# The last expert job of a hybrid decoder step on its own, and the work behind it

## What is computed

```python
def moe_swiglu(x, w_r, wg, wu, wd):
    logits = (x @ w_r).astype(jnp.float32)
    top_v, top_i = lax.top_k(logits, TOP_K)
    gates = jax.nn.softmax(top_v, axis=-1)
    dense_gate = jnp.sum(jax.nn.one_hot(top_i, N_EXPERTS, dtype=jnp.float32) * gates[..., None], axis=-2)
    out = jnp.zeros_like(x)
    for e in range(N_EXPERTS):
        out = out + dense_gate[..., e:e + 1].astype(x.dtype) * swiglu(x, wg[e], wu[e], wd[e])
    return out
    ...
    y = rmsnorm(x, P['ln_final'])
```

## Time and profile before

| | us |
|---|---|
| median of three runs | 1769.19 (1766.17 to 1771.72) |
| profiled execution | 1768.95 |
| its span | 1767.2 |
| TensorE busy | 1711.3 (97%) |
| VectorE busy | 1360.0 (77%) |
| ScalarE busy | 1054.7 (60%) |
| GpSimd busy | 111.5 (6%) |

### The profile page before, as it was taken

One profiled execution on the slowest core, in us unless ns is written; L12 is line 12 of the kernel. 1 busy time (PEld: TensorE's weight loads), 2 busy tenths in 40 slices (PEclk: granted clock), 3 DMA queues, 4 the chain that ended last, 5 costly groups with the idle time before them and its releaser, 6 DMA issues.

```text
span 1767.2 us, 24181 instructions
## 1 busy us (share of the span) xinstructions
PE 1711.3 (97%) x9024; PEld 1442.6 (82%) x9024; DVE 1360.0 (77%) x1383; ACT 1054.7 (60%) x1013; POOL 111.5 (6%) x119
## 2 busy tenths in 40 slices
PE   7999999999999999999999999999999999999995
PEld 5877899999787789788788788788787888887884
DVE  3679766664357975788888888988888888888885
ACT  2535544443243554677776776776777777776763
POOL 2054000000105400000000000000000000000000
PEclk9999999999999999899999999999999999999997
DMA  8455355546545535599899899999998998998990
GB/s 255 141 193 179 121 167 167 171 135 196 157 143 194 178 120 167 202 361 355 326 358 353 327 354 346 335 356 324 356 362 309 367 359 310 367 357 314 367 359 27
DMA packets 257027, 465.45 MB, mean 263 GB/s; under 512 B 8492, under 2 KB 108196, under 8 KB 256928
## 3 DMA queue, kind: packets, MB, share of 16 engines
q1 hardware_dynamic: 250288, 442.20, 72.1%
q0 software_dynamic: 6384, 21.28, 3.5%
q10 hardware_dynamic: 288, 1.08, 0.2%
HBM read 453.70 MB, written 11.15 MB: 263 GB/s over the span
## 4 chain that ended last, share of the span: by engine, by line
PE 87%; DVE 8%; ACT 3%; issue 2%; DMA 0%; DVEq 0%; POOL 0%; ACTq 0%; POOLq 0%
PE bank L872 84%; PE bank L876 3%; DVE arena L1728 2%; DVE w_lo L1731 1%; ACT w_hi L1383 1%; DVE moe_rows L1728 1%; ACT arena L1383 1%; DVE fw_lo L1731 1%; ACT fw_hi L1383 1%; DVE ysb_lo L1728 0%; DVE cs_t L1731 0%; DVE arena L1731 0%; DVE sam_y L1820 0%; DMA arena<-in_x_sample 0%; DVE bank L1942 0%
## 5 line engine op out<-in xcount | busy, mean ns | idle before, releaser
L1731 DVE TENSOR_TENSOR w_lo<-wring,w_hi 128x2048 fp32r<-128x2048 f32 x336 | 768.4, 2291 | 108.4 <-ACT w_hi L1383 107.6
L1383 ACT ACTIVATE w_hi<-wring 128x2048 fp32r<-128x2048 f32 x336 | 644.3, 1920 | 249.5 <-PE bank L872 249.4
L872 PE MATMUL bank<-w_hi,xg_hi 128*128 128x512 f32 x896 | 357.4, 399 | 13.4 <-DVE w_lo L1731 11.8
L872 PE MATMUL bank<-w_hi,xg_lo 128*128 128x512 f32 x896 | 353.3, 394 | 0.0
L872 PE MATMUL bank<-w_lo,xg_hi 128*128 128x512 f32 x896 | 352.5, 393 | 0.0
L872 PE MATMUL bank<-hn,wring 128*128 128x264 f32 x1152 | 267.4, 390 | 8.9 <-DVE hn L1728 6.5
L872 PEld LDWEIGHTS bank<-hn,wring 128*128 128x128 f32 x1152 | 217.5, 191 | 51.3 <-issue 12.1
L872 PEld LDWEIGHTS bank<-w_hi,xg_hi 128*128 128x128 f32 x896 | 168.3, 188 | 54.2 <-DVE w_lo L1731 15.3
L872 PEld LDWEIGHTS bank<-w_lo,xg_hi 128*128 128x128 f32 x896 | 168.4, 188 | 38.1
L872 PEld LDWEIGHTS bank<-w_hi,xg_lo 128*128 128x128 f32 x896 | 168.5, 188 | 36.2
L872 PE MATMUL bank<-w_hi,at_hi 128*128 128x512 f32 x448 | 177.8, 397 | 0.0
(11 more groups left out here) (260 smaller groups left out, 2065.2 us busy)
## 6 DMA issues: line engine op xcount, KB each, us to landing
wring<-in_moe_w_gate SPq DMA_DIRECT2D x112, 1024.0 KB, 5.2
wring<-in_moe_w_up SPq DMA_DIRECT2D x112, 1024.0 KB, 5.3
wring<-in_moe_w_down SPq DMA_DIRECT2D x112, 1024.0 KB, 5.0
wring<-in_w_in SPq DMA_DIRECT2D x36, 1024.0 KB, 5.4
wring<-in_w_out SPq DMA_DIRECT2D x16, 1024.0 KB, 5.3
wring<-in_ffn_w_gate SPq DMA_DIRECT2D x11, 1024.0 KB, 5.5
wring<-in_ffn_w_up SPq DMA_DIRECT2D x11, 1024.0 KB, 5.4
wring<-in_ffn_w_down SPq DMA_DIRECT2D x16, 704.0 KB, 4.7
```

What stands on the lines that cost most here:

```text
L872: return nc.tensor.matmul(out, lhsT, rhs, start=start, stop=stop)
L1383: return nc.scalar.activation(out, in_, fn, **kw)
L1731: return V.tensor_tensor(out, in0, in1, op)
```

## The change

- TensorE's loop runs over seven jobs. The eighth is a copy of its own (`job(NE - 1, last=True)`), without the gather behind it. ScalarE and VectorE leave out their parts of that gather (`high_slots`, `next_low_slots`) and VectorE the choice of slots (`choose`); with more than eight jobs all this is done after the branch.
- TensorE, ScalarE and VectorE read the number of jobs before the last job, not after it.
- In the last down products of the last job the last 12 are ordered by halves (`by_half`); `y0_full` tells ScalarE that the first half is complete, so that it makes `ysb_hi` of that half.
- `scatter_last` scatters by halves, as `ysb_ready` and the new `ylo_ready` come; VectorE adds the quarters in the order 0, 1, 2, 3, where 1 waits for the third fill and 2 for the second.
- ScalarE takes a root of `eps` right behind the last results, then waits for `y_free`; its square of the sample tile no longer waits for an addition.
- The sample tile is multiplied by `gfin` on GpSimd and scaled on ScalarE; VectorE makes its reciprocal. Tile 1 is scaled in two halves.
- The stores are issued from SP in the order tile 0, samples, first and second half of tile 1.

The diff without semaphore declarations and GpSimd's and SP's unchanged parts:

```diff
 # SP, behind the last load
+            sp.wait_ge(tile_ready[0], 1)
+            sp.dma_start(o[0][0, 0:P, :], outt[:, 0, :]).then_inc(y_out, 16)
+            sp.wait_ge(tile_ready[2], 1)
+            sp.dma_start(o[1].rearrange("b a d -> (b a) d"), outt[P - NB:P, 2, :]).then_inc(y_out, 16)
+            for h in range(2):
+                sp.wait_ge(tile_ready[1], h + 1)
+                hs = slice(512 * h, 512 * h + 512)
+                sp.dma_start(o[0][0, P:2 * P, hs], outt[:, 1, hs]).then_inc(y_out, 16)
+            sp.wait_ge(y_out, 64)
 # GpSimd
-            for i, t in enumerate((2, 0, 1)):
-                pool.wait_ge(y_ready, i + 1)
...
+            pool.wait_ge(acc_done, 1)
+            nc.gpsimd.tensor_tensor(outt[ROWS[2], 2, :], acc[ROWS[2], 2, :], gfin[ROWS[2], :], ALU.mult
+                                    ).then_inc(sam_weighed, 1)
 # TensorE
+            def down(s, j, p, n, by_half=False):
                 pe.wait_ge(evac[T_BANK], moe0[T_BANK] + n + 1)
...
+                for u in range(2):
+                    pe.wait_ge(lo_ready, j * PER_JOB + p + u + 1)
+                    order = ((0, 0), (1, 0), (0, 1), (1, 1)) if by_half else ((0, 0), (0, 1), (1, 0), (1, 1))
...
+                        if by_half and (u, i, h) == (1, 1, 0):
+                            ins.then_inc(y0_full, 1)
...
+            def scatter_last(n):
+                for h in range(2):
+                    hs = slice(512 * h, 512 * h + 512)
+                    pe.wait_ge(ysb_ready, 2 * n - 1 + h)
+                    for t in range(2):
+                        mm(bank[TAIL_BANKS[2 * t + h]][:, :], sct[:, t, :], ysb_hi[:, hs], start=True, stop=False)
+                    pe.wait_ge(ylo_ready, 2 * n - 1 + h)
+                    for t in range(2):
+                        mm(bank[TAIL_BANKS[2 * t + h]][:, :], sct[:, t, :], ysb_lo[:, hs], start=False, stop=True
+                           ).then_inc(tail_full, 1)
...
-            with pe.Fori(0, NE) as j:
+            with pe.Fori(0, NE - 1) as j:
                 job(j)
             pe.wait_ge(passes_ready, 1)
             jobs = nc.values_load(passes[0:1, 0:1], engines=[PE], min_val=NE, max_val=JOBS)
+            job(NE - 1, last=True)
             with nc.If(jobs > NE):
+                next_slots(NE - 1)
                 with pe.Fori(NE, JOBS) as j:
                     job(j)
+                scatter_last(JOBS)
             with nc.Else():
-                pe.wait_ge(passes_ready, 1)
-            pe.wait_ge(y_free, jobs + 1)
-            for p in range(4):
-                scatter(bank[TAIL_BANKS[p]], p).then_inc(tail_full, 1)
+                scatter_last(NE)
 # ScalarE
+                    if p == PER_JOB + SPLITS - 1:
+                        act.wait_ge(evac[S_BANK], moe0[S_BANK] + (j + 1) * S_FILLS)
+                        if last:
+                            act.wait_ge(y0_full, 1)
+                            high_result(0)
...
+            def last_results(n):
+                f(ssum[:, 0:1], eps[:, :], ACT.Sqrt)
+                act.wait_ge(y_free, n + 1)
...
+            act.wait_ge(sam_weighed, 1)
+            act.wait_ge(sam_scale, 1)
+            r = ROWS[2]
+            f(outt[r, 2, :], outt[r, 2, :], scale=ssum[r, 2:3]).then_inc(tile_ready[2], 1)
 # VectorE
-            for p in range(4):
-                dve.wait_ge(tail_full, p + 1)
+            for p, filled_by in ((0, 1), (1, 3), (2, 2), (3, 4)):
+                dve.wait_ge(tail_full, filled_by)
                 add_back(bank[TAIL_BANKS[p]], p).then_inc(acc_done, 1)
...
+            V.reciprocal(ssum[ROWS[2], 2:3], ssum[ROWS[2], 2:3]).then_inc(sam_scale, 1)
+            for t in range(2):
+                dve.wait_ge(act_step, 2 * t + 4)
+                link(V.reciprocal(ssum[:, t:t + 1], ssum[:, t:t + 1]))
+                for hs in (slice(0, D),) if t == 0 else (slice(0, D // 2), slice(D // 2, D)):
+                    stt(outt[:, t, hs], acc[:, t, hs], ssum[:, t:t + 1], gfin[:, hs], ALU.mult, ALU.mult
+                        ).then_inc(tile_ready[t], 1)
```

More of the change, by code:

```diff
@@ L560, in trunk @@
         ysb_ready = sem("ysb_ready")
-        y_ready = sem("y_ready")
+        y0_full = sem("y0_full")
+        ylo_ready = sem("ylo_ready")
+        tile_ready = [sem(f"tile_ready{t}") for t in range(3)]
+        sam_weighed = sem("sam_weighed")
+        sam_scale = sem("sam_scale")
         gfin_landed = sem("gfin_landed")
@@ L1320, in slots_back, with next_slots, ready, job @@
                 ins.then_inc(full[S_BANK], 1)
-            def job(j):
+            def next_slots(j):
+                pe.wait_ge(selm_ready, j + 2)
+                def ready(i):
+                    b = X_BANKS[i]
+                    pe.wait_ge(evac[b], moe0[b] + j)
+                    return bank[b]
+                gather(ready, lambda ins, i: ins.then_inc(full[X_BANKS[i]], 1))
+            def job(j, last=False):
                 for s in range(STEPS):
@@ L1341, in job @@
                 transposes(STEPS - 1, j * STEPS + STEPS - 1)
[L1343 to L1351, removed]
+                if not last:
+                    next_slots(j)
+                down(STEPS - 1, j, STREAM.index(("d", STEPS - 1, 0)), j * STEPS + STEPS - 1, by_half=last)
+            def scatter_last(n):
[8 more added lines that the diff above has]
+                           ).then_inc(tail_full, 1)
             pe.wait_ge(xs_ready, 2)
-            with pe.Fori(0, NE) as j:
+            with pe.Fori(0, NE - 1) as j:
                 job(j)
@@ L1650, in _, with high_slots, high_result, job @@
                 f(ex[:, t, :], ex[:, t, :], ACT.Exp, scale=rstd[:, t:t + 1]).then_inc(lexp_ready, 1)
-            def job(j, more):
-                for p in range(SPLITS, PER_JOB + SPLITS):
+            def high_slots(j):
+                for i, b in enumerate(X_BANKS):
+                    act.wait_ge(full[b], moe0[b] + j + 1)
+                    high_part(i)
+            def high_result(h):
+                f(ysb_hi[:, 512 * h:512 * h + 512], bank[Y_BANKS[h]][:, :], scale=gslot[:, :]).then_inc(ysb_ready, 1)
+            def job(j, more, last=False):
+                for p in range(SPLITS, PER_JOB + SPLITS):
+                    if p == PER_JOB + SPLITS - 1:
[3 more added lines that the diff above has]
+                            high_result(0)
                     if p < PER_JOB:
@@ L1669, in job @@
                         f(at_hi[:, (STEPS - 1) % 2], bank[T_BANK][:, :]).then_inc(at_hi_ready, 1)
-                        for i, b in enumerate(X_BANKS):
-                            act.wait_ge(full[b], moe0[b] + j + 1)
-                            high_part(i)
+                        if not last:
+                            high_slots(j)
                     if p == PER_JOB + SPLITS - 1:
[L1674 to L1677, removed]
+                        for h in range(1 if last else 0, 2):
+                            high_result(h)
                     if p >= PER_JOB and more:
                         split(j, p)
+            def last_results(n):
+                f(ssum[:, 0:1], eps[:, :], ACT.Sqrt)
+                act.wait_ge(y_free, n + 1)
             with act.Fori(0, NE - 1) as j:
                 job(j, True)
-            job(NE - 1, False)
             act.wait_ge(passes_ready, 1)
             jobs = nc.values_load(passes[0:1, 0:1], engines=[ACTE], min_val=NE, max_val=JOBS)
+            job(NE - 1, False, last=True)
             with nc.If(jobs > NE):
@@ L1688, in _ @@
                     split(NE, p)
+                high_slots(NE - 1)
                 with act.Fori(NE, JOBS - 1) as j:
@@ L2215, in low_part, with next_low_slots, job @@
                    ).then_inc(evac[T_BANK], 1)
-            def job(j, more):
+            def next_low_slots(j):
+                for i, b in enumerate(X_BANKS):
+                    dve.wait_ge(xg_hi_ready, 2 * j + 2 + i + 1)
+                    low_slots(i, bank[b]).then_inc(evac[b], 1)
+            def job(j, more, last=False):
                 for p in range(SPLITS, PER_JOB + SPLITS):
```

46 lines of the change are left out of this document (20 added, 26 removed).

## The result

Timed side by side, the changed kernel takes 1761.64 us (median of 9 runs, 1754.5 to 1762.8) and the kernel before 1766.17 (9 runs, 1764.16 to 1771.72). The ratio is 0.9948, 95% interval 0.9932 to 0.9964: 9.2 us less, between 6.4 and 12.0. This ratio is not that of the two medians, which would be 0.9974 (4.5 us) and lies outside the interval: the nine runs of the changed kernel fall into two groups, four from 1754.5 to 1756.8 and five from 1761.6 to 1762.8, and their median is one of the upper group. The means differ by 7.8 us. Which figure is nearest has to come from the traces. The profiled execution takes 1762.06, its span 1760.3.

A forecast was written before the change was run, and what follows sets the result against it. TensorE was taken to bound the kernel (87% of the span), with the change acting on the last job's end. The terms summed to 6.5 us, 1769.19 - 6.5 = 1762.7 us; stated range 1760.4 to 1766.4.

The forecast's parts named there:

- Gather gone: Last job, before its last down products: without the gather, down starts at about 1737.27 instead of 1738.87 us; gain 1.6.
- Results by halves: Last 12 down products reordered by halves: y_free 2.45 us after the last product instead of 3.86; gain 1.4.
- Scatter and the jump: After y_free: scatter hidden under VectorE's work, gap to the first addition taken as 0.35 us, bounds 0.1 and 1.56.
- rival A: Tail: the jumps stay on the path and SP's stores start slowly; gain 4.0 us or a little less, 1765.4; chance 0.22.
- Norm: Final norm: table load early, sample tile off VectorE; VectorE ends at 1752.0 us against 1758.05, 6.0 including earlier steps.
- Stores: Output stores issued from SP instead of GpSimd: last byte at 1754.4 us against 1760.9, gain 6.5 in all.
- The ending: After the last data: the 6.30 us without work stay; GpSimd's own waits worth 0 to 0.4, taken as 0.
- Reading early: Number of jobs read between jobs 7 and 8: cost taken as nothing, at most 1.35 us.
- Rival B: Boundary between jobs 7 and 8: the early read costs 0.75 to 2.7 us, time 1763.5 to 1765.4; chance 0.09.
- Rival C: Last job's TensorE code, never run before, must be fetched: costs 6.8 to 19.7 us, time 1769.4 to 1782.2; chance 0.06.

## Why the prediction was wrong, step by step

- **Gather gone**: 1.6 foreseen, 1.58 measured between the kernels, 1.68 with it put back alone. Right, with the wait for the low part in its place (1.75 [<-DVE at_lo], 1.9 foreseen).
- **Results by halves**: 1.4 foreseen for y_free, 1.33 measured. Right as a step, but alone it is worth 0.31 of tail, because the jump runs beside it.
- **Scatter and the jump**: the step that failed towards too much. It took the gap at 0.35 "near the low end, since that row is the nearest"; the row was the loop's end, where nothing has to wait for far code. The gap is 1.39. The branch on VectorE is indeed decided 1.7 us before the engine is done, as the prediction's idea of branches running ahead says, but 2.9 us pass until its target's first instruction; and it had been 1.5 us ahead already, with the read behind the job. The early read took 0.85 us off VectorE's gap (2.24 without it), and the shorter last results took away most of the cover again. The upper bound, 1.56, was near the truth. That is the one half of rival A, which read the fetch on q8 and the rule of the Trainium skill rightly: a fetch at a jump, of which engine work hides only a part. The early read is worth 0.76 us of tail beside the halves, and no more.
- **Norm**: the order was right (table load ahead of the first square, norm without a pause on ScalarE after it). ScalarE's jump was put at "about 0.5"; it held the table load up to E + 2.75 instead of E + 1.3. The first square came at E + 4.26 (2.9 foreseen), VectorE's end at E + 10.26 (8.95), 1.3 late. GpSimd's multiplication took 2.36 (1.9 foreseen, from a shape four times as many partitions high) and cost nothing.
- **Stores**: 2.4 us from VectorE's end to the last data foreseen, 2.7 measured. An issue on SP of about 0.4 was right (0.37 and 0.42).
- **The ending**: the 6.30 us "stay", and what GpSimd's own waits add "is worth between 0 and 0.4, and I take 0". This is the step that failed and put the time outside the range: the term was taken at nothing and was worth 5.4. The row showed a stretch without work, and I read it as a fixed cost of any kernel. GpSimd's DRAIN of 5.46 us was in the same trace, starting at 1761.5, 0.6 behind the last data; that it waits for the landing is shown by the one added wait (5.06 us).
- **Reading early**: 0 foreseen at the boundary, 0 measured (1.46 with and without). Rival B does not hold. That the jobs as a whole got 0.6 us longer was in no term.
- **Rival C**, TensorE's cold code: the last job's first product at 1627.23 and its last transposes at 1738.26 are 111.03 us apart; before (1623.90 to 1734.94) it is 111.04. Nothing was paid.

The sum: 6.5 foreseen, less 1.04 (jump), 0.2 (norm) and 0.4 (landing), more 5.4 (ending) is 10.3, and 10.2 were measured in the tail. With the ending as foreseen the gain would have been 4.9, 1.6 less than forecast, and 4.3 with the jobs' 0.6. Two errors partly hid each other: that the measured gain lies only 2.7 above the forecast is luck. The low end of the range was no bound of the sum either. It stands for a gain of 8.8, where the prediction's own upper bounds add up to 7.8; the rest was allowed for the scatter of runs.

## To carry to other kernels

Ask of every stretch at the end of a program which engine's last instruction it is: a wait for the output's landing belongs on an engine whose drain is short, and here GpSimd's took 5.2 to 5.5 us behind the landing where SP's took 0.013, so GpSimd should be done early. A branch near the critical path should fall through in the likely case; where it can't, what stands behind it should be put ahead of it (a table load, here), and a gain that ends at such a jump is given back. Where a program's early part scatters by more than the change is worth, compare the trace from a fixed point behind it.

## What the runs showed of the hardware

- GpSimd's DRAIN takes 5.2 to 6.1 us where nothing of its own is still running (5.46 before, 5.54, 5.21 and 6.10 in three versions), whether it issued the output's stores or not. In the changed kernel the record is 7.64, which starts with the multiplication and ends 5.3 behind it. What the engine does in this time the traces don't show. In the kernel before with SP's stores it stands at 708.3 us, takes 6.1 us and costs nothing:

```profile
L259 POOLq DRAIN  x1: 6097/6097/6097, 708.3 to 708.3; - x1
```

- From the taken branch at the end of the jobs to the first instructions where it leads it is 2.8 to 2.9 us on ScalarE and VectorE, and 0.3 from the branch back in VectorE's loop. On TensorE one instruction record covers it, 3.64 us after the change, hidden beside the down products:

```profile
L1395 PEldq COMPARE_BRANCH  x1: 3643/3643/3643, 1742.1 to 1742.1; - x1
```

- Reading one number into a register took 0.48 us on TensorE, 0.49 on ScalarE and 0.55 on VectorE, and 0.20 to 0.26 for the checks behind it.
- GpSimd needs 2.36 us for 32 x 1024 where 128 x 1024 took 1.91; fewer partitions did not make it faster. The two differ in their operands, and nothing here tells why it is slower.
